# Convolution projections as three f32r products, with the queries projected ahead of the keys

## What is computed

```python
q, k, v, qi, ki, wi, bg, cg, h = project(rmsnorm(x, g_mix), w_in)
a = sparse attention of q over the 256 keys that the indexer (qi, ki, wi) selects
def conv_mixer(bg, cg, h, prev, conv_w):
    u = cg * h
    up = concatenate([prev, u], axis=1)
    y = up[:, 0:t] * conv_w[0] + up[:, 1:1+t] * conv_w[1] + up[:, 2:2+t] * conv_w[2]
    return bg * y, up[:, -2:]
x = x + concatenate([a, b]) @ w_out
x = x + square(relu(rmsnorm(x, g_mlp) @ w_up)) @ w_down
```

## Time and profile before

| | |
|---|---|
| median of 3 runs | 1791.22 us (1790.99 to 1791.55) |
| the profiled execution, its own time | 1795.57 us |
| its span, first to last instruction | 1793.8 us |
| TensorE busy | 1710.6 us, 95% of the span |
| VectorE, ScalarE, GpSimd busy | 868.6, 635.2, 572.7 us |
| mean granted TensorE clock | 0.986 of 2.4 GHz |
| L1327 (q, cg, h and bg units) | 768 records, 236.9 us |
| DMA | 152.63 MB, mean 85 GB/s |

### The profile page before, as it was taken

How to read it: one execution, slowest core, us unless ns; L and a number is a source line. 1 busy time by engine, 2 the same in 40 slices (tenths; PEclk the granted TensorE clock), 3 DMA queues, 4 the chain that set the end, 5 groups by cost and what they waited for, 6 DMA issues and landing times.

```text
span 1793.8 us, 28526 instructions
## 1 busy us (share of the span) xinstructions
PE 1710.6 (95%) x10888; PEld 1352.8 (75%) x10888; DVE 868.6 (48%) x1920; ACT 635.2 (35%) x1336; POOL 572.7 (32%) x715
## 2 busy tenths in 40 slices
PE   7898999999999889999899999999999999999998
PEld 5553345656666556666555799999999999999997
DVE  4571888884765556777413342323232323232424
ACT  4464687545504444444311021212121212211223
POOL 1100233233426777776231302222222213040400
PEclk9898999999999999999999999999999999999999
DMA  8301031111027776776820002011111111111102
GB/s 248 96 6 48 31 117 50 36 36 43 1 75 210 219 217 207 218 205 185 284 98 0 1 1 94 2 51 43 47 47 47 47 47 47 47 47 47 59 1 100
DMA packets 66866, 152.63 MB, mean 85 GB/s; under 512 B 9290, under 2 KB 25406, under 8 KB 66512
## 3 DMA queue, kind: packets, MB, share of 16 engines
q1 hardware_dynamic: 45392, 79.55, 13.5%
q0 software_dynamic: 21376, 71.75, 13.4%
HBM read 140.61 MB, written 10.66 MB: 84 GB/s over the span
## 4 chain that ended last, share of the span: by engine, by line
PE 77%; issue 8%; DVE 8%; POOL 4%; DMA 2%; ACT 1%; DVEq 0%; SPq 0%; ACTq 0%
PE psum L1327 8%; PE psum L1741 7%; PE psum L1742 7%; PE psum L1754 7%; PE psum L1740 7%; PE psum L1752 7%; PE psum L1753 7%; PE psum L1681 7%; POOL arena L843 4%; PE psum L1466 2%; PE psum L1288 2%; PE psum L1614 2%; PE psum L1578 2%; PE psum L1600 1%; PE psum L1263 1%
## 5 line engine op out<-in xcount | busy, mean ns | idle before, releaser
L1740 PE MATMUL psum<-n_hi,wup_hi 128*128 128x384 f32 (+1 forms) x768 | 251.4, 327 | 0.0
L1741 PE MATMUL psum<-n_lo,wup_hi 128*128 128x384 f32 (+1 forms) x768 | 250.9, 327 | 0.0
L1742 PE MATMUL psum<-n_hi,wup_lo 128*128 128x384 f32 (+1 forms) x768 | 250.9, 327 | 0.0
L1752 PE MATMUL psum<-h_hi,wdn_hi 128*128 128x384 f32 (+1 forms) x768 | 250.9, 327 | 0.0
L1754 PE MATMUL psum<-h_hi,wdn_lo 128*128 128x384 f32 (+1 forms) x768 | 250.2, 326 | 0.0
L1753 PE MATMUL psum<-h_lo,wdn_hi 128*128 128x384 f32 (+1 forms) x768 | 250.1, 326 | 0.0
L2354 DVE TENSOR_TENSOR h_lo<-h_full,h_hi 128x384 fp32r<-128x384 f32 (+1 forms) x96 | 113.9, 1199 | 260.1 <-ACT h_hi L1169 250.0
L1327 PE MATMUL psum<-arena 128*128 128x384 f32 (+1 forms) x768 | 236.9, 469 | 0.0
L2359 DVE TENSOR_TENSOR x_region<-psum,x_region 128x384 f32<-128x384 f32 (+1 forms) x192 | 102.8, 536 | 252.9 <-PE psum L1754 252.5
L1161 ACT ACTIVATE hrelu<-psum 128x384 f32<-128x384 f32 (+1 forms) x96 | 45.5, 474 | 500.1 <-PE psum L1742 500.1
L1327 PEld LDWEIGHTS psum<-arena 128*128 128x128 f32 x768 | 144.9, 190 | 85.5
(11 more groups left out here) (317 smaller groups left out, 2598.5 us busy)
## 6 DMA issues: line engine op xcount, KB each, us to landing
wup_full<-in_w_up SPq DMA_DIRECT2D x8, 2048.0 KB, 8.0
wdn_full<-in_w_down SPq DMA_DIRECT2D x8, 2048.0 KB, 8.0
arena<-in_x_prompt SPq DMA_DIRECT2D x16, 512.0 KB, 10.3
arena<-in_w_in SPq DMA_DIRECT2D x3, 2048.0 KB, 8.4
arena<-in_w_in SPq DMA_DIRECT2D x12, 512.0 KB, 5.3
out<-arena SPq DMA_DIRECT2D x17, 256.0 KB, 6.9
arena<-in_w_out SPq DMA_DIRECT2D x8, 512.0 KB, 12.9
out<-arena SPq DMA_DIRECT2D x8, 512.0 KB, 2.6
```

The lines of the kernel that those rows point to most:

```text
L1740: pe.matmul(b, wu_hi[:, k, col], n_hi[:, k, o:o + w], start=(k == 0), stop=False)
L1741: pe.matmul(b, wu_hi[:, k, col], n_lo[:, k, o:o + w], start=False, stop=False)
L1742: i = pe.matmul(b, wu_lo[:, k, col], n_hi[:, k, o:o + w], start=False, stop=(k == KT - 1))
L1752: pe.matmul(b, wd_hi[:, f, col], h_hi[:, hf, 0:w], start=(f == 0), stop=False)
```

## The change

The 288 float32 matmuls of the cg, h and bg units become 864 f32r matmuls. ScalarE makes the high parts (`high_part`), GpSimd the low parts (`low_part`), of the activations (9 token tiles) and of the weights (12 blocks of 128 channels). The high activations lie where the queries and V lie, the low ones take the place of `nT`, and the high weights take the unused fourth quarter of each slab. So the queries are projected before the keys, the queries and V wait in memory and come back before attention, and the sample queries are kept apart in `qsmp`. Several semaphores are merged to make room for new ones; that changes no order.

```diff
 UNITS += [("v", t, "act") for t in range(NT)]
+UNITS += [("q", (j, c), "act") for j in range(4) for c in range(3)]
 for t in range(NT):
     UNITS.append(("k", t, "act"))
...
-UNITS += [("q", (j, c), "act") for j in range(4) for c in range(3)]
...
-LAST_OF_SLAB = {2: ("k", NT - 1), 3: ("q", (3, 2)), 4: ("bg", (0, 2)), 5: ("bg", (1, 2))}
+LAST_OF_SLAB = {2: ("q", (3, 2)), 3: ("k", NT - 1), 4: ("bg", (0, 2)), 5: ("bg", (1, 2))}
+def passes_after(kind, x):
+    return {"v": 2, "q": 1 + (kind == "q" and x[1] == 1), "k": 1 + (kind == "k" and x % 2),
+            "cg": 9 * (kind == "cg" and x[1] == 2)}.get(kind, 0)
+SPLITS = [("n", t) for t in range(NT - 2)] + [("w", 0), ("n", NT - 2), ("n", NT - 1)] + [("w", g) for g in range(1, 12)]
+for g in range(1, 12):
+    LO_AFTER.setdefault(passes_before(("cg", (g // 3, 2)) if g % 3 else ("h", (g // 3 - 1, 0))), []).append(("w", g))
...
 # SyncE, behind the stores of V
+            for j in range(4):
+                sp.wait_ge(pj_act, UCNT[UPOS[("q", (j, 2))]])
+                sp.dma_start(qscr[:, j, :], mixT[:, j, 0:SEQ]).then_inc(q_out, 16)
+            sp.wait_ge(pj_ready, UPOS[LAST_OF_SLAB[2]] + 1)
+            load_slab(4)
...
-            sp.wait_ge(pj_ready, UPOS[("bg", (2, 2))] + 1)
+            sp.wait_ge(pj_ready, UPOS[("h", (3, 2))] + 1)
             near_page(0, 1, ck, kring, near_in[0], k_used)
             sp.wait_ge(pj_ready, len(UNITS))
+            sp.wait_ge(q_out, 64)
+            sp.dma_start(mixT[:, 0:4, 0:2 * P], qscr[:, :, 0:2 * P]).then_inc(q_back[0], 16)
             sp.wait_ge(bt_out, 16)
             sp.dma_start(nbias, ...).then_inc(nbias_in, 16)
+            sp.dma_start(mixT[:, 0:4, 2 * P:SEQ], qscr[:, :, 2 * P:SEQ]).then_inc(q_back[1], 16)
+            sp.wait_ge(vst, 16 * NT)
+            sp.dma_start(V[:, 0:NB, :], vp.rearrange("(t p) c -> p t c", p=P)).then_inc(v_back, 16)
+            sp.dma_start(V[0:SMP, NB, :], vs).then_inc(v_back, 16)
...
 # GpSimd, in the loop of next_candidate
+            def low_part(kind, x):
+                pool.wait_ge(hi_made, SPLIT_NO[kind, x])
+                if kind == "n":
+                    o, w = TILES[x]
+                    pool.wait_ge(pj_ready, UPOS[("k", x)] + 1)
+                    for e in range(2):
+                        i = pool.tensor_tensor(nh_lo[:, 4 * e:4 * e + 4, o:o + w], nT[:, 4 * e:4 * e + 4, o:o + w], nh_hi[e][:, :, o:o + w], ALU.subtract)
+                else:
+                    i = pool.tensor_tensor(slab_r[w_home(x)], slab[w_home(x)], w_hi(x), ALU.subtract)
+                i.then_inc(lo_made, 1)
...
                     next_candidate(it, g)
+                    for kind, x in LO_AFTER.get(2 * (it + 1) + g + 1, []):
+                        low_part(kind, x)
...
 # ScalarE
+            def high_part(kind, x):
+                if kind == "n":
+                    o, w = TILES[x]
+                    if x == 0:
+                        act.wait_ge(q_out, 64)
+                        act.wait_ge(vst, 16 * NT)
+                    act.activation(nh_hi[0][:, :, o:o + w], nT[:, 0:4, o:o + w], ACT.Copy)
+                    act.activation(nh_hi[1][:, :, o:o + w], nT[:, 4:8, o:o + w], ACT.Copy).then_inc(hi_made, 1)
+                else:
+                    if x % 3 == 0:
+                        act.wait_ge(slab_in[4 + x // 3], 48)
+                    if x == 1:
+                        act.wait_ge(pj_ready, UPOS[("k", NT - 1)] + 1)
+                    if x >= 2:
+                        act.wait_ge(pj_ready, UPOS[(KINDS[(x - 2) % 3], ((x - 2) // 3, 2))] + 1)
+                    act.activation(w_hi(x), slab[w_home(x)], ACT.Copy).then_inc(hi_made, 1)
...
             for u in range(NE, len(UNITS)):
+                if kind == "cg" and x[1] == 0:
+                    high_part("w", 3 * x[0] + 1)
                 unit(u)
+                if kind == "k":
+                    if x == NT - 2:
+                        high_part("w", 0)
+                    high_part("n", x)
                 if kind == "cg" and x[1] == 2:
-                    more = 8
+                    high_part("w", 3 * x[0] + 2)
+                if kind == "h" and x[1] == 0 and x[0] < 3:
+                    high_part("w", 3 * x[0] + 3)
+                more = passes_after(kind, x)
                 for n in range(passes, min(passes + more, NPASS)):
                     sign_pass(n)
...
 # TensorE, units cg, h and bg
+                        if c == 0:
+                            pe.wait_ge(lo_made, SPLIT_NO["w", g])
+                        if (kind, x) == ("cg", (0, 2)):
+                            pe.wait_ge(lo_made, SPLIT_NO["n", NT - 1])
+                        w_lo = slab_r[w_home(g)]
+                        for k in range(KT):
+                            n_hi_, n_lo_ = nh_hi[k // 4][:, k % 4, o:o + w], nh_lo[:, k, o:o + w]
+                            pe.matmul(b[:, 0:w], w_hi(g)[:, k, :], n_hi_, start=(k == 0), stop=False)
+                            pe.matmul(b[:, 0:w], w_hi(g)[:, k, :], n_lo_, start=False, stop=False)
+                            i = pe.matmul(b[:, 0:w], w_lo[:, k, :], n_hi_, start=False, stop=(k == KT - 1))
...
 # TensorE, attention: logits(p, c), values(q)
+                if p in (0, 8):
+                    pe.wait_ge(q_back[p // 8], 16)
+                if q == 0:
+                    pe.wait_ge(v_back, 32)
```

More of the change, by code:

```diff
@@ L390, in build @@
         krow = v3(krow_, a=2)
+        place(-top[0] % 8)
         W0 = top[0]
@@ L428, in up8, with w_home, w_hi @@
             return (x + 7) // 8 * 8
+        nh_hi = [v3(at(f"nh_hi{i}", p, 4 * TOK, F32R), a=4) for i, p in enumerate((MIXAT, up8(VAT)))]
+        nh_lo = v3(at("nh_lo", NTAT, KT * TOK, F32R), a=KT)
+        def w_home(g):
+            return slice(None), (g // 3) % 2, slice(None), slice(g % 3 * P, g % 3 * P + P)
+        def w_hi(g):
+            return slab_r[:, g % 2, :, 3 * P:4 * P]
         krep = at("krep", up8(KRAT + 256), 2 * P, F32R).rearrange("p (s a d) -> p s a d", s=2, a=4)
@@ L589, in build @@
         yst = sem("y_stored")
+        q_out, v_back, q_back = sem("q_out"), sem("v_back"), [sem("q_back_first"), sem("q_back_rest")]
         gmix_in, x_scaled = sem("gmix_in"), sem("x_scaled")
@@ L713, in _ @@
                 sp.dma_start(rows_of(kp, ks, t), krow[0:TILES[t][1], t % 2, :]).then_inc(kst[t % 2], 16)
-            for n in range(4, 8):
+            for n in range(5, 8):
                 sp.wait_ge(pj_ready, UPOS[LAST_OF_SLAB[n - 2]] + 1)
@@ L1303, in unit @@
                 elif kind in ("v", "k"):
-                    s = int(kind == "v")
                     if x == 0:
-                        pe.wait_ge(slab_in[2 - s], 16)
+                        pe.wait_ge(slab_in[1 if kind == "v" else 3], 16)
                     o, w = TILES[x]
                     for k in range(KT):
-                        i = pe.matmul(b[0:w, :], nT[:, k, o:o + w], slab[:, s, k, :], start=(k == 0), stop=(k == KT - 1))
+                        i = pe.matmul(b[0:w, :], nT[:, k, o:o + w], slab[:, 1, k, :], start=(k == 0), stop=(k == KT - 1))
                 elif kind == "kt":
@@ L1405, in key_bits @@
             def key_bits():
[L1407 removed]
+                pe.wait_ge(rank_in, 32)
                 pe.wait_ge(mask_bits, 1)
```

84 lines of the change are left out of this document (46 added, 38 removed).

## The result

The changed kernel takes 1826.14 us (1824.17 to 1827.18) against 1791.38 (1790.99 to 1791.57): ratio 1.0193, 95% interval 1.0175 to 1.0211. It is 35 us slower, 24 more than the 11 of the sum. Its profiled execution is the fastest of four: 1824.17 us with a span of 1822.4, 28.6 above the 1793.8 of before.

A forecast was written before the change was run, and what follows sets the result against it. TensorE was taken to bound the projections, with VectorE's mask a fixed point and VectorE bounding the tail. +11 (s) - 9 - 1 + 5 (c) + 5 (a) = +11 us on 1791.2 gave 1802 us, range 1783 to 1820.

The forecast's parts named there:

- the sum: Whole kernel: all terms together, 11 us slower, 1802 us on the median; slower by more than 3.6 us had chance 0.64.
- the term from M to list 7: From VectorE's mask end (M) to the end of key_list(7): 120 us against 129.3, 9 us gained, bounds 2 and 24.
- The term a: Attention's start: returning queries and V delay the first product with V, 5 us lost, bounds 0 and 13.
- s: Before the mask: GpSimd's splits hold up VectorE's two-input steps, 11 us lost, bounds 0 and 30.
- c: After TensorE's long stalls: dense work runs at half clock for some 4 us each, 5 us lost, bounds 0 and 10.
- rival (3): Collisions and returns weigh full: s = 20, gain 5 from mask to list 7, c = 8, a = 10; 1824 us, chance 0.13.
- TensorE's saving: Projections: a triple takes 11.9 us instead of some 14.7; twelve save 34 us of TensorE, a ceiling.
- The walk's 8: Before the mask: walking down both queues with unchanged times gave 8 us of delay, four pairs falling into counts whole.
- the chain of 33.6 us for w6: Before group 2: ScalarE's evacuation, high parts, nine sign passes, waits and GpSimd's low part, 33.6 us; TensorE stalls 8.
- The chain for w9: Before group 3: the same work with seven passes and two waits, 29 us against TensorE's 26.6; a stall of 2.
- The tail: From list 7 to the last evacuation: VectorE's 28.1 us of work sets the pace, 1 us gained (-1 to 2.4).
- Costed at nothing: The q stores, ScalarE's wait for q_out, its k-unit work and the untouched MLP were taken to cost 0.

The follow-up runs named there:

- the reordered kernel: The changed kernel's new order and parking of queries and V, but projections in plain float32 without high and low parts: 1800.12 us, ratio 1.0045.
- the two experiments that take away either side: Two edits of the changed kernel: no token low parts subtracted on GpSimd, 1817.21 us; VectorE's five tiny two-input steps rewritten as one-input tensor_scalar, 1822.52 us.
- the first experiment: The changed kernel with the high parts of w3, w6 and w9 made inside the burst of sign passes, low parts behind the next candidate: 1801.71 us, ratio 1.0054.
- the run of three: The changed kernel with split inside the burst, V returned ahead of the queries' rest, and one-input tiny steps together: 1789.86 us, ratio 0.9985.

## Why the prediction was wrong

The sign was right (slower, 0.64), the mechanisms were mostly the ones named, and the sum was short by 17.5 of 28.5 us. The step that failed is the term from M to list 7, forecast at -9 and measured at +10.3. The term a was short by 6.5, s was 2.7 too high, and the 5 us of c lie inside the legs. The time lies where rival (3) put it, but not by its numbers: it had s = 20 and a gain of 5 from M to list 7.

**TensorE's saving.** Right. The first triple ran from 347.01 us to 359.06, 12.0 us against the 11.9 of the sum, at 0.176 and 0.147 us a matmul.

**s, the mask.** 8.3 us against 11, within its bounds. The walk's 8 hit that number by luck: against the reordered kernel the cost is 10.7, near the 11, and the new order gave 2.4 back, which no term had. The mechanism, VectorE's tiny two-input steps behind GpSimd's subtractions, is shown by the two experiments that take away either side and by the held steps' 10.8 us. The estimate took every collision for one with a tie bit; four of the 13 held steps stand ahead of the first.

**From M to list 7.** Here the sum failed: the forecast gained 9 us, 10.3 were lost. Its first step was 30 us from the mask to the end of cg(1,2). ScalarE began that evacuation at 417.52, 36.6 us after the mask: list 0 waited 3.39 us instead of 1.5, and TensorE ran at half clock behind the mask and again behind list 0. The second step was the chain of 33.6 us for w6. It took 36.8 (417.5 to 454.3): the nine passes took 24.0 us of the forecast 23.8 and ScalarE's waits were as forecast (3.50 and 0.53), but the low part was taken to follow its high part. In the code `low_part` comes behind the candidates of the burst's last two passes, and one of them met a one_hot. That is 3.9 us between the high part's end and 451.88. Then the triple cg(2) took 15.0 us to its last evacuation, with 3.6 us at clock 0.50. The chain for w9 was forecast at 29 us (its terms add up to 28.3) and took 36.6 (469.3 to 505.9): 8.7 us of waits (4.52, 0.45 and 3.69) for two of 2.76, and 4.6 of GpSimd's candidates again. The mechanism was right, the stalls of 8 and 2 us were 11.35 and 9.00. Within the two chains there were two errors. One was the order in GpSimd's queue, 3.9 and 4.6 us. The other was to copy the one wait that the earlier trace rows showed, 2.76 us: a one_hot product holds GpSimd for up to 4.4 us, and a burst met two or three of them. The experiment on GpSimd's order alone gives that part 4 us, that on the whole split 25 in this leg.

**The clock (c).** 5 us in total was right, by the balance of the first experiment, and one of the places was wrong. Behind the mask, where the wait is longest, keeping the clock up gained 2.3 us up to list 0 and 0.4 up to list 7. The clock costs behind list 0 (1.2 us), behind the two stalls (2.1 and 1.8), and once more at attention's start, counted there.

**The tail.** 0.9 us gained against 1. TensorE now waits 4.36 us for VectorE at the transposes, where before it worked through to the end.

**Attention's start (a).** 11.5 us against 5, within the bounds of 13. The wait for V is 7.85 of it, where I had put the stall at up to 7. The rest is mostly that TensorE enters at half clock after the 4.36 us (0.50 from 549.4 to 557.4 us), and 1.6 us of waiting for gathers that start later. The stretch from the first return's issue to the product, and its densest part:

```profile
551.13:582.30 31.17, 19.11 (x195) 13.83 (x194) 11.05 (x51) 8.32 (x19) 14.55 (x16) 0.77 0.92 317
...
557.50:576.00 18.50, 13.48 (x158) 9.62 (x157) 8.63 (x34) 6.53 (x16) 9.27 (x11) 0.91 1.02 371
```

The rate of 297 GB/s was too low: 317 were moved on average. But they carried 9.9 MB where the sum had 8.3, 6.1 on SyncE's queue and 3.7 for the gathers against 5.3 and 3. So it was the volume that I had underrated. The Trainium skill's 358 GB/s (SBUF — State Buffer, section A bandwidth-pool intuition that's wrong) lies above the 317 of the whole stretch and below the 371 of its densest part, so there the measurement goes beyond the page. By 358 I had estimated 2 us for this term; with 9.9 MB in place of 8.3 the same working gives an estimate of 6, so it was the volume that misled it, not the rate.

**Costed at nothing.** It held: the stores of q, the wait for `q_out` and the MLP show no loss. In the reordered kernel alone the only new waits are the 7.46 us for V and 1.4 for a gather.

## What to carry to other kernels

When work is inserted into an in-order queue, its price is the position, not the duration: write down what stands ahead of it there, and what each of those waits for in turn. Here 2.4 us of subtraction, placed behind a burst of search steps instead of inside it, cost 24 us. A wait that is seen once in a trace is a sample, so bound it by the instruction that causes it (4.4 us), not by the sample (2.8 us). And when a bound engine gets faster, ask at each of its waits which engine sets that moment: of some 34 us that the new products save TensorE, the mask, the splits and V's return kept all.

## What the runs showed of the hardware

A 128 x 1 step of VectorE with two SBUF tensors took 0.16 us alone and up to 2.20 beside a GpSimd subtraction, ending with it. The same step as tensor_scalar with a per-partition operand took 0.21 us in every one of its 73 records from 284 to 377 us, beside the subtraction or not; with two such operands its mean was 0.27. A tensor_scalar of 128 x 64 took 0.25 us alone and 2.38 beside the subtraction. The lock works both ways: GpSimd's 128 x 2 steps, 0.2 us alone, took 4.4 us beside one_hot's product, and its 2.4 us subtraction 5.08. In these records the one that started first kept its time: one_hot's product kept its 4.4 us in all eight records of the changed kernel, and took 5.39 in the run of three where a subtraction had begun 1.3 us before it.
